# Feed-forward of an attention block: gate and up as seven block products too, with the inner product kept in memory

## What is computed

```
h  = rms_norm(x, norm_mix_g);   x2 = x + nsa_mixer(h, ...)     # attention, untouched by the change
h2 = rms_norm(x2, norm_ffn_g)
y  = x2 + (silu(h2 @ wg) * (h2 @ wu)) @ wd                     # wg, wu 2048 x 5632, wd 5632 x 2048
```

## Time and profile before

| | |
|---|---|
| median of 3 runs | 2321.43 us (2320.02 to 2321.55) |
| the profiled execution | 2319.32 us, span 2317.5 us |
| TensorE busy | 99% of the span, 11963 matmuls |
| VectorE / ScalarE / GpSimd busy | 56% / 34% / 3% |
| granted TensorE clock, mean | 0.995 |
| moved from memory | 223.55 MB read, 4.19 MB written |

### The profile page before, as it was taken

How to read it: one execution, slowest core, us unless ns; L and a number is a source line. 1 busy time by engine, 2 the same in 40 slices (tenths; PEclk the granted TensorE clock), 3 DMA queues, 4 the chain that set the end, 5 groups by cost and what they waited for, 6 DMA issues and landing times.

```text
span 2317.5 us, 30952 instructions
## 1 busy us (share of the span) xinstructions
PE 2291.8 (99%) x11963; PEld 1968.9 (85%) x11963; DVE 1304.8 (56%) x1993; ACT 777.8 (34%) x1163; POOL 76.2 (3%) x89
## 2 busy tenths in 40 slices
PE   8999999999999999999999999999999999999998
PEld 7898988889889999888888888888888888888886
DVE  5333466565665556456554646565565646464647
ACT  4332344443453434322222223223322223232322
POOL 1000000000010000000000000000000000000000
PEclk9999999999999999999999999999999999999999
DMA  5343211222123113255353544535443535253444
GB/s 162 114 118 88 77 52 49 64 61 67 53 67 128 64 65 101 88 167 146 95 152 99 152 121 118 146 109 146 118 136 109 146 96 152 90 153 119 127 109 136
DMA packets 225456, 252.81 MB, mean 109 GB/s; under 512 B 14172, under 2 KB 188273, under 8 KB 224161
## 3 DMA queue, kind: packets, MB, share of 16 engines
q1 hardware_dynamic: 218050, 222.36, 30.2%
q0 software_dynamic: 7264, 28.51, 6.4%
HBM read 223.55 MB, written 4.19 MB: 98 GB/s over the span
## 4 chain that ended last, share of the span: by engine, by line
PE 96%; DVE 2%; ACT 1%; issue 0%; DMA 0%; POOL 0%; SPq 0%; ACTq 0%; DVEq 0%
PE ps L1261 93%; PE ps L1569 2%; DVE wl L759 1%; ACT wh L455 0%; DVE x_rows L773 0%; PE ps L1559 0%; PE ps L1605 0%; DVE x_rows L1182 0%; DVE hTl L759 0%; DVE down L1157 0%; DMA down<-in_ffn_w_down_dram 0%; DVE pbuf L1043 0%; PE ps L1308 0%; ACT x_rows L455 0%; ACT hTh L455 0%
## 5 line engine op out<-in xcount | busy, mean ns | idle before, releaser
L1261 PE MATMUL ps<-hTh,wh 128*128 128x512 f32 (+1 forms) x1968 | 763.5, 388 | 2.4 <-DVE wl L759 1.8
L1261 PE MATMUL ps<-hTh,wl 128*128 128x512 f32 (+1 forms) x1968 | 759.6, 386 | 0.0
L1261 PE MATMUL ps<-hTl,wh 128*128 128x512 f32 (+1 forms) x1968 | 759.2, 386 | 0.0
L759 DVE TENSOR_TENSOR wl<-raw,wh 128x1024 fp32r<-128x1024 f32 x298 | 363.0, 1222 | 347.4 <-ACT wh L455 345.6
L455 ACT ACTIVATE wh<-raw 128x1024 fp32r<-128x1024 f32 x298 | 314.3, 1059 | 534.5 <-PE ps L1261 420.3
L1261 PEld LDWEIGHTS ps<-hTh,wh 128*128 128x128 f32 x1968 | 369.8, 188 | 75.5 <-issue 2.2
L1261 PEld LDWEIGHTS ps<-hTh,wl 128*128 128x128 f32 x1968 | 369.6, 188 | 75.0
L1261 PEld LDWEIGHTS ps<-hTl,wh 128*128 128x128 f32 x1968 | 369.9, 188 | 72.3
L759 DVE TENSOR_TENSOR wl<-down,wh 128x1024 fp32r<-128x1024 f32 x132 | 161.3, 1222 | 157.0 <-ACT wh L455 157.0
L1261 PE MATMUL ps<-wh,opsh 128*128 128x512 f32 x616 | 240.8, 391 | 6.1 <-DVE x_rows L1182 4.3
L1261 PE MATMUL ps<-wl,opsh 128*128 128x512 f32 x616 | 240.2, 390 | 0.0
(11 more groups left out here) (181 smaller groups left out, 2019.3 us busy)
## 6 DMA issues: line engine op xcount, KB each, us to landing
raw<-in_ffn_w_gate_dram SPq DMA_DIRECT2D x176, 256.0 KB, 3.0
raw<-in_ffn_w_up_dram SPq DMA_DIRECT2D x176, 256.0 KB, 3.0
down<-in_ffn_w_down_dram SPq DMA_DIRECT2D x176, 256.0 KB, 3.2
raw<-in_nsa_w_in_dram SPq DMA_DIRECT2D x164, 256.0 KB, 3.0
raw<-in_nsa_w_out_dram SPq DMA_DIRECT2D x64, 256.0 KB, 3.0
t<-in_ffn_w_down_dram SPq DMA_DIRECT2D x44, 256.0 KB, 3.3
down<-down POOLq DMA_DIRECT2D x22, 512.0 KB, 6.0
t<-down POOLq DMA_DIRECT2D x22, 512.0 KB, 6.1
```

The lines of the kernel that those rows point to most:

```text
L759: nc.vector.tensor_tensor(dst, src, hi.bitcast(f32), ALU.subtract).then_inc(done, 1)
L1261: return nc.tensor.matmul(out_, a, b, start=start, stop=stop, skip_group_check=True)
```

## The change

The feed-forward becomes two phases of **turns**. Turns 0 to 10 (`up`) are one slab of 512 hidden columns each, with the seven-product scheme over [gate | up]: the two column blocks b are gate and up, the two row blocks k are halves of each four k-tiles of 128, the two token blocks are halves of 256. The stationary operands are token blocks and their sums (`left_hi`/`left_lo`, made once), and the weights move, so that a turn has 7 products j of 4 units u, 12 matmuls a unit. The result m comes with tokens in the partitions; it is transposed back by TensorE (`m_tiles`, 16 transposes a turn), its block sums are made (`m_combine`) and all seven are stored to memory (`m_dram`). Turns 11 to 18 (`down`) are four chunks of 3, 3, 3 and 2 slabs, each for two halves of the output columns: 7 products of 3 (or 2) units. Their stationary operands are read back from `m_dram` one tile of 128 x 512 at a time (77 tiles) and split. `x2` is stored to memory (`x2_dram`) before the first turn and read back, in two DMAs of 2 MB, in turn 11.

The weights' sums of both phases are now: one of the four by VectorE (`sum_a`), three by GpSimd as TENSOR_TENSOR of 128 x 1024 (`tb`, `tc`, `td`). The ring of split weights is three deep. The gains are put on at the evacuation of the transposed tiles, `norm_bcast` goes, and the root-mean-square factor is a scalar per partition in the silu and in the product. Results of the seven products are combined by accumulation in PSUM and by operations between copies in `works` (q1, s5, s7, s56 by ScalarE; w, c22, v, c21, c12 by VectorE), and four adds per down turn bring them into `x2`.

```diff
-SLABS, G_UNITS, QUAD, DOWN = 11, 16, 7, 14      # MIXED: "g" and "d" units interleaved, ring of 4
+CHUNKS = [(0, 3), (3, 6), (6, 9), (9, SLABS)]
+DOWN0, TURNS, PRODUCTS, RING3 = SLABS, DOWN0 + 2 * len(CHUNKS), 7, 3
 # gpsimd
-            for turn in range(2 * SLABS):
-                pool.dma_start(down[:, 1, :], down[:, 0, :], accum_op=ALU.add)
-                pool.dma_start(t3[:, :], down[:, 3, :], accum_op=ALU.add)
+            for c in range(4):
+                pool.wait_ge(x2b_added, 4 * c + 4)
+                pool.dma_start(x2_dram[:, :, c * 512:(c + 1) * 512], x2[:, :, c * 512:(c + 1) * 512])
+            for t in range(TURNS):
+                for u in range(U):
+                    pool.wait_ge(loaded1[u], ...); pool.wait_ge(loaded2[u], ...)
+                    pool.wait_ge(ta_done, sums + u + 1)
+                    pool.tensor_tensor(g1[u][:, :], g1[u][:, :], g2(t)[u][:, :], ALU.add).then_inc(tb_done, 1)
+                for u in range(U):
+                    pool.wait_ge(lo_ready, unit_at(t, 2, u) + 1)
+                    pool.tensor_tensor(g1[u][:, :], g1[u][:, :], g0[u][:, :], ALU.add).then_inc(tc_done, 1)
+                for u in range(U):
+                    pool.wait_ge(lo_ready, unit_at(t, 3, u) + 1)
+                    pool.wait_ge(loaded0[u], 64 * (t + 1))
+                    pool.tensor_tensor(g1[u][:, :], g1[u][:, :], g0[u][:, :], ALU.add).then_inc(td_done, 1)
 # scalar: high(t, j, u)
+                # j = 1 waits for ta, j = 2 for tb, j = 3 for tc, j = 5 for td
+                act.wait_ge(units_used, n - RING3 + 1 ...)
+                copy(wh[:, slot, :], src).then_inc(hi_ready, 1)
 # scalar, per position of a turn
+                    high(t, pos // U, pos % U)
+                    if (t, pos) in FORM: copy(down_hi[j][:, u, :, :], formed[f % STAGES][:, :, :])
+                    # mT copies at 7 and 11; s5, q1, s7, s56 at 12, 13, 18, 19 (up); silu at 24, 27 and 0
 # vector
+            def sum_a(t, u):
+                dve.wait_ge(units_used, n - RING3 + 1)
+                nc.vector.tensor_tensor(sum_a_val[:, (n - F0) % RING3, :], g0[u][:, :], g1[u][:, :], ALU.add)\
+                    .then_inc(ta_done, 1)
+                for pos in range(PRODUCTS * U):
+                    if j == 1: sum_a(t, u)
+                    low(t, j, u)
+                    if (t, pos) in FORM: lo(down_lo[fj][:, fu, :, :], ...)      # 128 x 512
+                    # up: products at 1 and 3, c12 at 2, m_combine at 8 and 12,
+                    #     w, c22, v at 20 to 22, c21 at 26
+                    # down: c21, y21, c12 at 0 to 2, y12 at 2U, w, c22, y22, v, y11 at 16 to 20
 # tensor, per unit
+                    for tt in range(2):
+                        for i in range(2):
+                            mm3(bank(2 * into + tt), (hi[:, u, i, ts], low[:, u, i, ts]),
+                                (wh[:, slot, at], wl[:, slot, at]), ...)
+                    last.then_inc(units_used, 1)
 # sync
+            sp.wait_ge(x2_spilled, 64) ...          # before the first loads into x2's place
+                    if t == DOWN0 and pos == 1:   sp.dma_start(x_rows[:, 0:2, :], x2_dram[:, 0:2, :])
+                    if t == DOWN0 and pos == 14:  sp.dma_start(x_rows[:, 2:4, :], x2_dram[:, 2:4, :])
+                        if t == DOWN0 - 1: sp.wait_ge(units_used, unit_end(t, 6))
+                        weights(t + 1, 1, 1, u, g2(t + 1)[u], loaded2[u])
```

More of the change, by code:

```diff
@@ L33, with chunk_of, units_of, units_before @@
 SLABS = D_FF // 512
[L34 to L47, removed]
+CHUNKS = [(0, 3), (3, 6), (6, 9), (9, SLABS)]
+DOWN0 = SLABS
+TURNS = DOWN0 + 2 * len(CHUNKS)
+PRODUCTS = 7
+RING3 = 3
+def chunk_of(t):
+    return (t - DOWN0) // 2
+def units_of(t):
+    if t < DOWN0:
+        return KD // 4
+    first, end = CHUNKS[chunk_of(t)]
+    return end - first
+def units_before(t):
+    return sum(units_of(v) for v in range(t))
+def unit_at(t, j, u):
+    return F0 + PRODUCTS * units_before(t) + j * units_of(t) + u
+def unit_end(t, j):
+    return unit_at(t, j, units_of(t) - 1) + 1
+def pairs_of(t):
+    x, z, spare = 0, 1, 3
+    for _ in range(t):
+        x, z, spare = spare, x, z
+    return x, z, 2, spare
+LEFT_LO = [0, 4, 5, 1, 2, 3, 6]
+def forming():
+    at, f = {}, 0
+    for c, (first, end) in enumerate(CHUNKS):
+        t = DOWN0 - 1 if c == 0 else DOWN0 + 2 * c - 1
+        pos = 26 if c == 0 else 15
+        for j in range(PRODUCTS):
+            for u in range(end - first):
+                width = PRODUCTS * units_of(t)
+                at[(t, pos) if pos < width else (t + 1, pos - width)] = (c, j, u, f)
+                pos, f = pos + 1, f + 1
+    return at
+FORM = forming()
+FORMED = {v[:3]: v[3] + 1 for v in FORM.values()}
+STAGES = 4
 LAST = GROUPS - 1
@@ L376, in _, with weights @@
-            out_v = out[0].rearrange("(t p) d -> p t d", p=P)
[L377 to L380, removed]
+            def weights(t, k, b, u, dst, done):
+                if t < DOWN0:
+                    src = ((w_gate_v, w_up_v)[b])[u][:, 2 * k:2 * k + 2, t * 512:(t + 1) * 512]
+                else:
+                    col = (t - DOWN0) % 2 * 1024 + b * 512
+                    src = w_down_v[CHUNKS[chunk_of(t)][0] + u, k, :, :, col:col + 512]
+                at = dst[:, :].rearrange("p (i c) -> p i c", i=2)
+                for i in range(2):
+                    sp.dma_start(at[:, i, :], src[:, i, :]).then_inc(done, 16)
@@ new lines, in _ @@
+            for u in range(4):
+                if u < 2:
+                    sp.wait_ge(lo_ready, F0 - 1 + u)
+                else:
+                    sp.wait_ge(units_used, F0 - 2)
+                weights(0, 0, 0, u, g0[u], loaded0[u])
+            sp.wait_ge(units_used, F0)
+            for u in range(4):
+                weights(0, 0, 1, u, g1[u], loaded1[u])
+            sp.wait_ge(x2_spilled, 64)
+            sp.wait_ge(x2_sq, 16)
+            sp.wait_ge(h2T_banks, 16)
+            for u in range(4):
+                weights(0, 1, 1, u, g2_up[u], loaded2[u])
@@ L381, in _ @@
+            out_v = out[0].rearrange("(t p) d -> p t d", p=P)
+            for n in range(2):
+                done = TURNS - DOWN0 - 1 + n
+                for added, row, b in ((y22_added, 2, 1), (y11_added, 0, 0), (y21_added, 2, 0), (y12_added, 0, 1)):
+                    at = (slice(None), slice(row, row + 2), slice(n * 1024 + b * 512, n * 1024 + b * 512 + 512))
+                    sp.wait_ge(added, done)
                     sp.dma_start(out_v[at], x2[at]).then_inc(stored, 16)
@@ new lines, in _ @@
+            for c in range(4):
+                for n in (B0 + 2 * c + RING, B0 + 2 * c + 1 + RING):
+                    if n < F0:
+                        split(n)
+                if c:
+                    left_evacuate(c - 1)
+                    left_high(c - 1, LEFT_LO[:3])
+                squares(c)
+                if c:
+                    act.wait_ge(left_sums, c)
+                    left_high(c - 1, LEFT_LO[3:])
+            high(0, 0, 0)
+            high(0, 0, 1)
+            left_evacuate(3)
@@ new lines, in left_low, with low @@
+            def left_low(c, first, end):
+                dve.wait_ge(left_sums, c + 1)
+                for at in range(first, end):
+                    j = LEFT_LO[at]
+                    dve.wait_ge(left_his, PRODUCTS * c + at + 1)
+                    lo(left_lo[j][:, c, :, :], left_val[j][:, c, :, :], left_hi[j][:, c, :, :], left_los)
+            def low(t, j, u):
+                n = unit_at(t, j, u)
+                slot = (n - F0) % RING3
+                src = (g0[u], None, g1[u], g1[u], g0[u], g1[u], g2(t)[u])[j]
+                src = sum_a_val[:, slot, :] if j == 1 else src[:, :]
+                dve.wait_ge(hi_ready, n + 1)
+                lo(wl[:, slot, :], src, wh[:, slot, :], lo_ready)
@@ new lines, in c21, with c12 @@
+            def c21(t):
+                dve.wait_ge(units_used, unit_end(t, 5))
+                dve.wait_ge(v_done, t + 1)
+                w = works(t)
+                nc.vector.tensor_tensor(w[1][:, :, :], w[1][:, :, :], pair(pairs_of(t)[2]), ALU.add).then_inc(c21_done, 1)
+            def c12(t):
+                dve.wait_ge(units_used, unit_end(t, 6))
+                w = works(t)
+                dst = w[0] if t < DOWN0 else w[3]
+                nc.vector.tensor_tensor(dst[:, :, :], pair(pairs_of(t)[1]), w[0][:, :, :], ALU.subtract).then_inc(c12_done, 1)
@@ L1258, in _ @@
+            c21(TURNS - 1)
+            y21(TURNS - 1)
+            c12(TURNS - 1)
+            y12(TURNS - 1)
         @block.tensor
```

692 lines of the change are left out of this document (388 added, 304 removed).

## The result

The changed kernel takes 2444.39 us (median of 4 runs, 2443.38 to 2446.32) against 2321.13: ratio 1.0533, 95% interval 1.0521 to 1.0546. It is slower, as forecast, but by 123 us and not by 40, and outside the range. The profiled span is 2444.5 us; the sum of the prediction was 2357.2. Experiments given as "one run" were measured once; a kernel's repeated runs here spread by 2 to 7 us.

A forecast was written before the change was run, and what follows sets the result against it. The prediction took TensorE's number of matmuls as the bound. Entry 925.3 + TensorE's work 1277.2 + start 13 + up turns 75 + turn 11 8 + down turns 53 + tail 5.7 = 2357.2 span, forecast 2361 us, range 2228 to 2420.

The forecast's parts named there:

- the 528 matmuls less: Feed-forward, gate and up: 4224 matmuls become 3696 at 0.2266 us each, which removes 119.7 us.
- The exclusive port in both directions: SBUF port: a GpSimd add also makes VectorE's two-tile operations wait until it ends, up to 2.3 us; assumed, no row showed it.
- The price of an add: GpSimd's 198 adds of 128x1024: 2.3 us each, between bounds of 1.22 and 2.73; own range 2.0 to 2.7.
- The forced gap: Up turns, positions 4 to 7: tb takes the port while VectorE waits for ScalarE; 4.7 us per unit against 2.72, 5.0 stall.
- The sign: Whole kernel: slower by 1.7%, as 149 us of stalls eat a net saving of 100; chance of slower 0.56.
- The step that failed: Up turns, positions 8 to 15: adds slip behind VectorE's lows; only low 13 late by 0.2 us and low 15 by 1.5.
- The clock: TensorE's clock at the stalls: stalls of 1.2 to 2.0 us keep it, so the sum has nothing for it.
- After 925.3: Start of the feed-forward: TensorE enters at 925.3, then 13 us of stall, 11 at unit 3 and 2 for lost slack.
- The start of turn 11: Loads at turn 11: 2 us for the first loads, 3 us for each of two x2 reads, together 8 us.
- The first (no wait of VectorE): VectorE does not wait for GpSimd, so only GpSimd's adds are late: 2233 us, faster; chance 0.25.
- The second (short adds): Adds near 1.2 us: stalls 42 in place of 128, 2275 us, chance 0.12; break-even about 1.8 us an add.
- The third: TensorE's clock falls: if paid at each of some 60 stalls, 100 us more, 2460 us; chance 0.11.

The follow-up runs named there:

- Experiment 9: Changed kernel with td of the up turns waiting for the low of product 4 in place of product 3: 2402.0 us (one run), turn 85.8.
- experiment 1: Changed kernel with GpSimd's adds touching only 8 of the 1024 columns, all waits kept: 2267.43 us (one run), turn 79.0.
- experiment 3: Changed kernel with only tb moved to VectorE, tc and td staying on GpSimd: 2370.76 us (one run), turn 85.25.
- experiment 5: Changed kernel with zero filler matmuls in up turns ahead of units 5, 6, 7 (7 each) and 13 (15): 2431.82 us (one run), turn 88.3.

## Why the prediction was right in its mechanism and wrong in its size

**What held.** TensorE's pitch and the 528 matmuls less: with the adds off the port the scheme is 2.1 to 2.5% faster than before. The exclusive port in both directions, which had no row for one of them: shown by the lows that end 1.1 us after an add. The price of an add, 2.39 against 2.3. The forced gap: 4.79 us a unit against 4.7, and idle times at units 5 to 7 of 1.55, 1.75 and 1.76 against 1.2, 1.9 and 1.9. The sign, with its reason.

**The step that failed** is "VectorE then does two lows at once and keeps the port (as in rows 8), so that adds slip behind". When both have work waiting they take the port by turns. The longest run of it is in a down turn of the changed kernel, seven lows without a break on VectorE, and GpSimd's last three adds beside them:

```profile
2171.72 18.75 DVE L944 TENSOR_TENSOR wl<-g,wh 128x1024 fp32r<-128x1024 f32 x7 [0.23 <-ACT wh L583]
```

```profile
2177.03 10.08 POOL L577 TENSOR_TENSOR g<-g,g 128x1024 f32<-128x1024 f32 x3
```

Three adds take 10.08 us: each its 2.2 and one low of 1.13. So adds of positions 8 to 15 go in between VectorE's operations and not behind them, and even an `m_combine` operation of 0.42 us waits for a whole one. Experiment 9 shows it by moving four of the eight: 3.9 us a turn, 2.5 without the clock's part. The forecast had unit 13 late by 0.2 us and unit 15 by 1.5; in the trace unit 13 is late by 3.5 (in seven of ten turns) and unit 15 not at all. By experiments 1 and 3, positions 8 and after cost 6.3 us a turn with the clock, against my 1.7. Port and clock together cost 179 us, against 128 forecast: 51 of the 87 us that the sum lacks. Of these 179, 11 x 10.7 = 118 are in the up turns (75 forecast) and 61 in the rest (53 forecast).

**The clock.** I let it cost nothing, because my stalls were of 1.2 to 2.0 us and a stretch with 1.7 us of idle time kept it at 1.00. By the timeline of the kernel before, that was a stall of 1.73 us, and the one behind which it fell was of 2.40:

```profile
2268.00 0.47 PE L1261 MATMUL ps<-wh,opsh 128*128 128x512 f32 x1 [1.73 <-DVE opsl L759]
...
2276.13 0.76 PE L1261 MATMUL ps<-wh,opsh 128*128 128x512 f32 x1 [2.40 <-DVE x_rows L1182]
```

In most up turns the clock is lost to the stall of 3.5 us at unit 13, and so to the same failed step; in three of ten also behind stalls of 1.5 to 1.8 us, which in the other turns cost nothing. As a price it is small: about 1.5 us a turn by experiment 5, some 15 us of the 51. It falls in the down turns too (0.92 and 0.95 over turns 11 and 13), and no run holds it there. It goes away with the adds: it is 1.00 over the up turns of experiment 1. That it also moves the order at the port (a late unit 8 changes which add meets which low) makes the two parts inseparable below that.

**The other 36 us** are in the structure without the adds, as experiment 1 has it. TensorE enters the feed-forward at 931.0 and not at 925.3, 5.7 us: ahead of it `left_combine` and `left_low` stand in VectorE's list between the adds of the output projection, and TensorE waits for these; the step "After 925.3" took the entry from the kernel before, and did not count what was put ahead of it. An up turn takes 79.0 and not 77.9 even so, and a three-slab down turn about 59.3 and not 57.1. That is about 13 and 14 us. Part of it is that `sum_a`, high, low have no overlap at product 1: 3.5 us a unit in an up turn, 4.1 with the form low. I had these stalls only where an add was in the gap. In experiment 1 they make one wait of 0.5 us in an up turn, and 0.7, 1.1 and 1.1 in a down turn with form lows; the rest of the 13 and 14 us is not in TensorE's list of waits, and stays open. The start of turn 11 took somewhat less than forecast (8): 4.4 at the end of turn 10 (83.4 against 79.0) and about 2 after. The few us that are left are in the two-slab turns (40.4 to the next `sum_a`, forecast 38.1) and the tail.

**The rivals.** The first (no wait of VectorE) is out by the trace. The second (short adds) by their 2.39. Its break-even of 1.8 us an add was too high too: even adds of 8 columns leave the kernel only 52 us under the one before (2317.5 - 2265.7), where the forecast had 88; where the break-even lies, no run shows. The third happened, at a fraction of the price given. The range ended at 2420, set by the forecast's own bound of 2.7 us an add; it had no case for more adds in the path, though the port's own sum could have been its upper bound. As an estimate from the prediction's figures for positions 4 to 15: 16 operations of 1.13, eight of 0.42 and twelve adds of 2.3 are 49.0 us, against 34.4 that TensorE needs for twelve units and `m_tiles`, so up to 14.6 late. Over a whole turn the same sum (47.6 + 27.6 = 75.2) fits into 77.9 and warns of nothing.

**Open.** Why in the earlier trace rows three VectorE operations in a row went ahead of a waiting inverse root, while an add gets in after one. No run separates the kind of GpSimd operation from its size. Why the same three stalls lose the clock in three turns of ten and keep it in seven is open too.

## What to carry to other kernels

Before work goes to an idle engine, ask what it shares with the busy one: GpSimd at 3% was no spare capacity, since its adds and VectorE's two-tile operations are served one at a time, and the slower one holds twice as long. Where two engines share something, bound the time by the plain sum of both, over the stretch where both have work and not over the whole turn, then look for the places where a slow holder can enter a gap that the schedule forces on the fast one. A move pays by what it takes out of such a gap: filling it with the same add on VectorE gave 4.4 us a turn, and doing so for all adds turned 5.3% slower into 2.1% faster.

## What the runs showed of the hardware, unexpected

- A GpSimd memset of 128x1024 takes 0.955 us and runs beside VectorE's two-tile operations with no delay on either side; an add of the same tile takes 2.39 and excludes them.
- VectorE and GpSimd alternate at the port, one instruction each, when both wait: two halves of an add (1.28 us each undisturbed) let one VectorE operation in between, and all but the first unit of a turn's product 1 still take 4.77 us.
- Equal stalls do not always cost the clock. Three idle stretches of 1.55 to 1.77 us with 2.7 us of work between them were followed by 1.2 GHz in three turns of the changed kernel; in seven turns with the same three stalls, in nine of ten turns of experiment 9, and after four of 1.8 us in turn 0 (957.7 to 972.1), it stayed at 1.00.
